# Three edits to a hybrid mLSTM / Fourier diffusion step: TensorE's head loop written out, transform halves ahead of modulation tiles, residual stream in three parts

## What is computed

```python
mod = silu(c) @ w_mod + b_mod            # six vectors: sh1, sc1, g1, sh2, sc2, g2
h = x * (1 + sc1) + sh1
q, k, v, o, gt, uf, ga, gb = split(h @ w_in)
h_m, finals = mlstm_bidir(q, k, v, gates, init)          # 4 heads, chunked scans in both directions
y_a = (norm(h_m) * sigmoid(o)) @ w_branch_a
y_b = fourier(uf) @ w_branch_b                           # real part of a 2-D / 3-D DFT per channel group
merged = sigmoid(ga) * y_a + sigmoid(gb) * y_b
x = layer_norm(ALPHA * x + g1 * (merged @ w_out))
h2 = x * (1 + sc2) + sh2
a, u = split(h2 @ w_ffn_in)
x = layer_norm(ALPHA * x + g2 * ((silu(a) * u) @ w_ffn_out))
```

## Time and profile before

| | |
|---|---|
| runs of the kernel | 1375.59, 1379.22, 1385.62; median 1379.22 |
| profiled execution | 1376.62, of which the span of instructions is 1374.6 |
| mean granted TensorE clock | 0.997 |
| TensorE matmul busy | 1353.2 (98%) |
| VectorE, GpSimd, ScalarE busy | 848.7, 752.9, 466.9 |
| DMA | 164.66 MB, mean 120 GB/s |

### The profile page before, as it was taken

The page is one execution under the profiler, slowest core; times in us unless marked ns, Lnnn a source line. Parts: engine busy times, 40 slices in busy tenths (PEclk is TensorE's granted clock), DMA queues, the critical chain, the costliest instruction groups (busy, mean ns, idle before and its releaser), DMA issues.

```text
span 1374.6 us, 23148 instructions
## 1 busy us (share of the span) xinstructions
PE 1353.2 (98%) x8717; PEld 1289.5 (94%) x8717; DVE 848.7 (62%) x1446; ACT 466.9 (34%) x827; POOL 752.9 (55%) x420
## 2 busy tenths in 40 slices
PE   9999999999999999999999999999999999999997
PEld 7898999899899989989999999998999999988886
DVE  4766993257346635752686486487877777764307
ACT  5824222231231123122233100366555455553220
POOL 2455865623552363245235666456998889852440
PEclk9999999999999999999999999999999999999999
DMA  9634634212312321142137555723222222242321
GB/s 379 255 108 158 216 110 145 76 57 85 116 67 65 122 79 58 54 140 70 36 107 256 173 191 179 158 82 131 85 82 92 92 73 79 93 169 77 123 77 77
DMA packets 59697, 164.66 MB, mean 120 GB/s; under 512 B 8168, under 2 KB 22768, under 8 KB 58360
## 3 DMA queue, kind: packets, MB, share of 16 engines
q1 hardware_dynamic: 38856, 143.20, 30.7%
q10 hardware_dynamic: 20784, 20.69, 4.8%
HBM read 146.53 MB, written 17.34 MB: 119 GB/s over the span
## 4 chain that ended last, share of the span: by engine, by line
PE 72%; DVE 10%; issue 8%; POOL 5%; ACT 3%; DMA 2%; DVEq 0%; ACTq 0%; POOLq 0%; SPq 0%
PE psum L1467 19%; PE psum L994 15%; PE psum L1504 11%; PE psum L1357 8%; PE psum L1339 5%; PE psum L1087 4%; POOL w_hi L817 3%; PE psum L1211 2%; DVE nt_a L2438 2%; POOL w_lo L821 2%; PE psum L1295 2%; PE psum L1050 1%; DVE yl L2480 1%; DMA raw<-in_wunits 1%; PE psum L1258 1%
## 5 line engine op out<-in xcount | busy, mean ns | idle before, releaser
L817 POOL TENSOR_TENSOR w_hi<-raw,zero 128x1024 fp32r<-128x1024 f32 x80 | 153.5, 1919 | 385.8 <-PE psum L994 278.0
L821 POOL TENSOR_TENSOR w_lo<-raw,w_hi 128x1024 fp32r<-128x1024 f32 (+1 forms) x113 | 274.5, 2429 | 120.8 <-ACT w_hi L2150 73.4
L1467 PE MATMUL psum<-t_r,ws_r 128*128 128x322 f32 x1848 | 276.6, 311 | 2.0 <-POOL ws_r L894 0.7
L1467 PEld LDWEIGHTS psum<-t_r,ws_r 128*128 128x128 f32 x1848 | 275.1, 189 | 3.2 <-issue 2.0
L994 PE MATMUL psum<-h_hi,w_hi 128*128 128x256 f32 (+1 forms) x768 | 176.2, 310 | 1.2 <-PEq L1403 1.2
L994 PE MATMUL psum<-h_lo,w_hi 128*128 128x256 f32 (+1 forms) x768 | 174.9, 309 | 0.0
L994 PE MATMUL psum<-h_hi,w_lo 128*128 128x256 f32 (+1 forms) x768 | 174.8, 309 | 0.0
L894 POOL TENSOR_TENSOR ws_r<-ws_f,ws_r 128x512 fp32r<-128x512 f32 x88 | 124.4, 1414 | 33.4 <-DVE ws_f L2707 19.9
L994 PEld LDWEIGHTS psum<-h_hi,w_hi 128*128 128x128 f32 x768 | 137.8, 188 | 2.6 <-issue 1.9
L994 PEld LDWEIGHTS psum<-h_lo,w_hi 128*128 128x128 f32 x768 | 139.8, 188 | 0.0
L994 PEld LDWEIGHTS psum<-h_hi,w_lo 128*128 128x128 f32 x768 | 139.7, 188 | 0.0
(11 more groups left out here) (357 smaller groups left out, 3031.1 us busy)
## 6 DMA issues: line engine op xcount, KB each, us to landing
raw<-in_wunits SPq DMA_DIRECT2D x124, 512.0 KB, 3.4
pair<-in_wunits SPq DMA_DIRECT2D x46, 512.0 KB, 4.3
mod_slot<-in_wmod SPq DMA_DIRECT2D x16, 512.0 KB, 14.1
mod_ring<-in_wmod ACTq DMA_DIRECT2D x16, 512.0 KB, 3.4
yg_dram<-yg_sb ACTq DMA_DIRECT2D x20, 256.0 KB, 3.0
yg_st<-yg_dram SPq DMA_DIRECT2D x16, 320.0 KB, 3.6
c_raw<-in_stateC SPq DMA_DIRECT2D x4, 1028.0 KB, 7.0
z_ring<-in_wmod SPq DMA_DIRECT2D x8, 512.0 KB, 4.4
```

Of the source, the lines that this page charges most:

```text
L817: pool.tensor_tensor(hi, src, zero[:, 0:1].broadcast_to([P, src.shape[1]]), ALU.add)\
L821: pool.tensor_tensor(lo, src, hi.bitcast(F32), ALU.subtract).then_inc(w_split, 1)
L1467: ins = mm(out, ws_r[n][:, w, cols], t_r[:, n, k, x, :], start=(starts and k == 0 and m == 0), stop=(k == HALF_K - 1 and m == 2), skip_gro ...
```

## The change

Four places are touched, one in each of four engines' blocks, for three edits.

1. TensorE's `with pe.Fori(0, H) as h: head(h)` becomes a Python loop: the body is written out four times, and its waits compare with constants.
2. VectorE: `uf_mods(3)` moves behind the last `channels_rest` and the low half of `fn_r`.
3. The residual stream is loaded and scaled in three parts: k-tiles 0 and 4, then 1 and 5, then the other four. SyncE issues the first two where it issued both parts before, and the third behind the load of unit U_OUT+3, with a wait for the landing of the first on its semaphore. ScalarE has `upper(0)` ahead of the second scaling, and the third scaling behind `lower(0)`. VectorE waits for them one tile pair at a time.

```diff
             sp.wait_ge(units_done, U_OUT)
-            for n, part in enumerate((slice(0, 1), slice(1, HALF_K))):
+
+            def residual_in(part, n):
                 sp.dma_start(by_half(r_all[:])[:, :, part, :], by_half(xT)[:, :, part, :]).then_inc(xf_in[n], 16)
+
+            residual_in(slice(0, 1), 0)
+            residual_in(slice(1, 2), 1)
             weights_next(U_OUT + 3)
+            sp.wait_ge(xf_in[0], 48)
+            residual_in(slice(2, HALF_K), 0)
...
-            with pe.Fori(0, H) as h:
+            for h in range(H):
                 head(h)
...
-            def x_scaled(n, part):
+            def x_scaled(part, n, landed):
 
-                act.wait_ge(xf_in[n], 48)
+                act.wait_ge(xf_in[n], landed)
                 A_(by_half(r_all[:])[:, :, part, :], by_half(r_all[:])[:, :, part, :], ACT.Copy, scale=ALPHA)\
                     .then_inc(aug_hi_ok, 1)
...
-            x_scaled(0, slice(0, 1))
+            x_scaled(slice(0, 1), 0, 48)
             out_hi(2)
-            x_scaled(1, slice(1, HALF_K))
+            upper(0)
+            x_scaled(slice(1, 2), 1, 48)
             out_hi(3)
-            upper(0)
             lower(0)
+            x_scaled(slice(2, HALF_K), 0, 64)
             out_hi(4)
...
-            uf_mods(3)
             channels_rest(3)
             v.wait_ge(ft_hi_ok, 2 * NG + 1)
             lo_rows = slice(32, 64)
             sub(fn_r[lo_rows, :], psum[lo_rows, 6, 0:NR], fn_r[lo_rows, :]).then_inc(ft_ok, 1)
+            uf_mods(3)
...
-                if i == 0:
-                    v.wait_ge(aug_hi_ok, 3)
+                if i < 2:
+                    v.wait_ge(aug_hi_ok, 3 + i)
```

## The result

The changed kernel takes 1368.57 us (median of 5 runs, 1368.0 to 1369.62), the kernel before 1379.07 (5 runs, 1375.59 to 1385.62). The profiled execution of the changed kernel took 1369.62 (span 1367.6, clock 0.999) against 1376.62 before: 7.0 us, where the sum of the prediction had 6.8. So the sum fits the pair of profiled executions, and the medians lie 10.5 apart. Where the other 3.5 us are is taken up behind the experiments.

A forecast was written before the change was run, and what follows sets the result against it. TensorE's matmuls were busy 98% of the span, so its 21.4 us of idle time plus time lost to a lower clock bounded any gain. Terms 2.8 + 0 + 4.0 = 6.8 gave 1369.8, forecast 1371.0 us, range 1366.5 to 1377.

The forecast's parts named there:

- the sum of the prediction: Whole kernel: gains of 2.8 (transform order), 0 (head loop) and 4.0 (residual stream), together 6.8 us.
- the steps given: Transform's end: `fn_r` done at about 115.9, so TensorE's 2.9 us wait before `merged(0)` goes; 2.8 taken.
- Gain 0: Head loop written out: branches show no cost on TensorE's path, waits stay, added instruction fetches cost nothing.
- rival C: Heads 1 to 3: TensorE runs dry of instructions, some 20 blocks late; 1391 at 1 us each; chance 0.05.
- the taken branches in this trace show no stall: Head loop's jumps: no idle row at a taken branch, so removing them was taken to gain 0.
- rival A: Output projection: the stall moves on to U_OUT+4, leaving 0 to 2.5 of the residual gain; 1373 to 1375; chance 0.22.
- the 891.5 that the prediction asked for: Output projection: residual's last 1280 KB must land by 891.5 for U_OUT+4 to be split just in time, at 899.3.
- `out_hi(3)` once TensorE has left U_OUT+1: ScalarE, output projection: `out_hi(3)` runs 885.3 to 886.4, so the 2.2 us stall at U_OUT+3 goes.
- I add half of the 2.6: From profile to median: shown runs' median was 2.6 above the profiled execution; half added to 1369.8 gives 1371.0.

The follow-up runs named there:

- edit 3 alone: Kernel before with only the residual stream in three parts, with its scalings and `upper(0)` as in the change: 1374.70 us, ratio 0.9967.
- edit 1 alone: Kernel before with only TensorE's head loop written out: 1376.05 us, ratio 0.9977.
- Edit 2 alone: Kernel before with only `uf_mods(3)` moved behind the low half of `fn_r`, head loop kept: 1373.11 us, ratio 0.9953.

## Why the prediction was right, and where it was not

**Edit 2.** Gain 3.0 in the profile, 2.8 predicted, by the steps given. The tiles, the refill of tile 6 and `merged(1)` behaved as worked out, the last with more slack.

**Edit 1.** "Gain 0" held in the pair of profiles for the heads: none changed, three waits of 0.7 stayed, rival C didn't come. The wait behind the heads is ScalarE's `gate_a(3)`, as the prediction read it: in all 14 traces TensorE went on 0.3 us after that row's end. It was 0.9 longer in the first profile of the changed kernel, and 0.85 came back over the 16 mixing units, 7.04 us each and not 7.09. Neither comes from the change: with the loop the wait was 0.8 to 1.3 (and 2.2 in the loop of two heads), written out 0.5 to 2.4, and 7.04 occurs with and without it. What failed is the step "the taken branches in this trace show no stall": it was true of the one execution that it was read from, and the run of edit 3 alone shows 2.9 and 2.5 at the same jumps. The Trainium skill's rule (Runtime: NRT & Kernel Launch, "Instruction fetch mechanics"), that a taken branch to code outside the fetched window waits for a fetch, names this mechanism, and three jumps agree; at the other sixteen the trace shows neither a fetch nor a stall. Where the 2.9 us of edit 1 alone come from stays open. Its clocks give about 1.3 (0.9970 against 0.9961). Saved stalls could be the rest: 9 of 26 runs of the kernel before were above 1380 and none of the 12 with edit 1 alone. But none of the 21 runs with edit 2 or edit 3 alone was either, and both keep the loop; the nine long runs had a mean clock of 0.9949 against 0.9967 for the other seventeen, so their length is in part clock; and beside edits 2 and 3 the loop costs nothing measurable.

**Edit 3.** 4.0 predicted, 3.9 measured from the start of U_OUT+0 to the end of the span (503.6 before, 499.8 after), with other parts: 2.2 for the wait and 1.7 for the clock as predicted; 1.4 lost around U_OUT+4 (1.1 of wait, the rest small gaps), where the prediction had 0.1; 0.6 won at U_OUT+6 and U_OUT+7 and 0.9 from the FFN's start on, where it had 0.2 and a bound. The stall moved on as in rival A, at half its size and with no clock lost, but not for A's reason: the last 1280 KB had landed at 889.8, before the 891.5 that the prediction asked for. The step that failed is "`out_hi(3)` once TensorE has left U_OUT+1": TensorE had left it at 881.9, and the load landed at 885.5, 3.6 later. I had the slow stretch in the rows, moved 1280 KB out of the load's way, and took that for enough; what slowed it was the store beside it, which stayed.

**From the sum to the median.** This is the term that was mis-sized. "I add half of the 2.6" took the distance between the profiled execution and the median for noise that both kernels share. It is not, and part of it is a gain of the change. Over 62 runs of the kernel before the mean clock is 0.9962, over 18 of the changed kernel 0.9982, that is 0.0020 x 1373 = 2.8 us gained per execution, where the one profile showed 1.7. (The clock's fall after the last matmul is in these means too; it costs nothing, and in the 14 profiles it takes in the last 2.9 to 6.0 us of the span whatever the kernel.) Edit 2 alone shows 2.5, as the wait before `merged(0)` was followed by a stretch at 1.2 GHz in two of four profiles, and edits 1 and 3 alone 1.3 each; each is uncertain by about 0.5, and they don't add up to the 2.8. So of the 3.5 us by which the medians say more than the profiled pair, about 1.1 is clock, by this estimate. Another 1.05 is that the profiled execution of the changed kernel lay that much above its own median; its two waits of 2.1 and 1.1 were 0.5 and 0.7, 0.2 and 1.0 in the other two profiles. The last 1.4 is in runs of the kernel before that were longer than its profile, and stays open; stalls at the jumps are of that size, but were not shown in that kernel.

## What to carry to other kernels

One profile is one execution: a wait that costs its length in the trace may be followed by a stretch at half speed in another, and a loop's jump that is free in the trace may cost 3 us in another. Before an order is rearranged for a late load, look at what else the queues carry in that stretch, small pieces above all; and before a wait is removed by moving an instruction forward, read what refills its inputs release.

## What was not expected of the hardware

- TensorE's clock. In 14 profiles there are ten waits of 2.1 to 2.9 us behind TensorE's first matmul. Five of them, 2.2 to 2.8 long, were followed within 2 us by a stretch of 3.4 us at 1.2 GHz, which costs 1.7; five, 2.1 to 2.9 long, were not. No such stretch stands anywhere else before the last matmul, and none behind the many waits below 1.5 us. (The 2.2 us on `idle_r` in every trace lie ahead of the first matmul and aren't counted.)
- While a store of 8 KB in four-byte pieces was under way, 4 KB packets of the other queue took 1.2 us in place of 0.17 for some 10 us, most of that after the last small packet; the loads issued then took 7 to 9 us longer to land than without it.
- A loop body of 825 matmuls was kept in five of six profiled executions (no block fetched in later rounds). In the sixth it was fetched again at two of three jumps, with 2.9 and 2.5 us in which TensorE stood; a body of twice that length was fetched again at its one jump, with 1.1.
- The 16 mixing units ran at 7.04 us each in twelve traces and at 7.09 in two, the matmuls evenly stretched, in looped kernels only but not in all of them.
